# Seven block products for gate and up in three of four feed-forward blocks, with the weight sums on GpSimd

## What is computed

```python
D_FF = 2816

def swiglu(h, w1, w3, w2):
    return (jax.nn.silu(h @ w1) * (h @ w3)) @ w2

def _half_ffn(h, g, m, k, w1, w3, w2):
    y = swiglu(_modulate(h, g, m, k), w1, w3, w2)
    return h + (0.5 * m[:, :, 3 * k + 2] * y).astype(h.dtype)
```

## Time and profile before

| what | value |
|---|---|
| median of three runs | 2884.31 us |
| span of the profiled execution (its own total time is not listed) | 2881.4 us |
| granted TensorE clock, mean | 0.991 of full speed |
| TensorE busy | 2789.6 us, 97% |
| VectorE busy | 1520.7 us, 53% |
| ScalarE busy | 1126.3 us, 39% |
| GpSimd busy | 546.4 us, 19% |
| HBM read | 255.48 MB, 89 GB/s over the span |

### The profile page before, as it was taken

How to read it: one execution, slowest core, us unless ns; L and a number is a source line. 1 busy time by engine, 2 the same in 40 slices (tenths; PEclk the granted TensorE clock), 3 DMA queues, 4 the chain that set the end, 5 groups by cost and what they waited for, 6 DMA issues and landing times.

```text
span 2881.4 us, 40758 instructions
## 1 busy us (share of the span) xinstructions
PE 2789.6 (97%) x15696; PEld 2604.4 (90%) x15696; DVE 1520.7 (53%) x1919; ACT 1126.3 (39%) x1620; POOL 546.4 (19%) x264
## 2 busy tenths in 40 slices
PE   5999999999998999999999999999999999899999
PEld 5899999999986799999999999999998875788887
DVE  6974266564558668652664632222247657543332
ACT  3333134335547635331343422123324876532231
POOL 2442044210002522430442100000011520100000
PEclk8999999999999999999999999999999999999999
DMA  7443144212130014441442122212222110123232
GB/s 295 139 153 133 49 151 155 92 47 65 53 73 1 1 52 139 160 155 50 152 158 88 47 65 68 70 51 66 65 67 73 52 59 8 59 88 104 93 97 99
DMA packets 68391, 258.76 MB, mean 90 GB/s; under 512 B 7504, under 2 KB 9424, under 8 KB 67792
## 3 DMA queue, kind: packets, MB, share of 16 engines
q1 hardware_dynamic: 50736, 192.59, 20.3%
q10 hardware_dynamic: 17568, 65.02, 6.6%
HBM read 255.48 MB, written 2.10 MB: 89 GB/s over the span
## 4 chain that ended last, share of the span: by engine, by line
PE 86%; DVE 7%; issue 2%; ACT 2%; POOL 0%; DVEq 0%; POOLq 0%; ACTq 0%
PE banks L459 21%; PE banks L463 21%; PE banks L461 21%; PE banks L466 5%; PE banks L470 5%; PE banks L468 5%; DVE banks L1661 2%; PE banks L950 1%; PE banks L789 1%; DVE wl L1656 1%; PE banks L973 1%; DVE tmp L1849 1%; DVE xl L1841 1%; PE banks L873 1%; DVE nsS L2008 0%
## 5 line engine op out<-in xcount | busy, mean ns | idle before, releaser
L1079 ACT ACTIVATE wh<-raw 128x1024 fp32r<-128x1024 f32 (+1 forms) x300 | 338.8, 1129 | 1454.3 <-PE banks L463 1151.3
L459 PE MATMUL banks<-xh,wh 128*128 128x384 f32 x2608 | 671.6, 338 | 27.9 <-DVE wl L1656 15.8
L461 PE MATMUL banks<-xl,wh 128*128 128x384 f32 x2608 | 664.7, 335 | 0.0
L463 PE MATMUL banks<-xh,wl 128*128 128x384 f32 x2608 | 664.4, 335 | 0.0
L1656 DVE TENSOR_TENSOR wl<-raw,wh 128x1024 fp32r<-128x1024 f32 (+1 forms) x300 | 428.3, 1428 | 350.6 <-ACT wh L1079 349.8
L459 PEld LDWEIGHTS banks<-xh,wh 128*128 128x128 f32 x2608 | 471.7, 189 | 37.1 <-DVE wl L1656 19.0
L461 PEld LDWEIGHTS banks<-xl,wh 128*128 128x128 f32 x2608 | 473.9, 189 | 0.0
L463 PEld LDWEIGHTS banks<-xh,wl 128*128 128x128 f32 x2608 | 473.1, 189 | 0.0
L2419 POOL TENSOR_TENSOR mraw<-mraw,scb 128x1024 f32<-128x1024 f32 x120 | 316.1, 2635 | 636.2 <-DVE banks L1661 636.2
L463 PE MATMUL banks<-hh,wl 128*128 128x384 f32 x1056 | 267.9, 334 | 0.0
L461 PE MATMUL banks<-hl,wh 128*128 128x384 f32 x1056 | 267.9, 334 | 0.0
(11 more groups left out here) (368 smaller groups left out, 3240.4 us busy)
## 6 DMA issues: line engine op xcount, KB each, us to landing
raw<-in_w SPq DMA_DIRECT2D x176, 512.0 KB, 3.6
mraw<-in_wmn ACTq DMA_DIRECT2D x120, 512.0 KB, 4.4
raw<-in_w SPq DMA_DIRECT2D x64, 704.0 KB, 4.0
raw<-in_abin SPq DMA_DIRECT2D x24, 512.0 KB, 3.6
raw<-in_cdin SPq DMA_DIRECT2D x20, 512.0 KB, 3.6
mini<-in_wmn SPq DMA_DIRECT2D x9, 512.0 KB, 14.8
gmini<-in_wmn SPq DMA_DIRECT2D x2, 2048.0 KB, 21.8
raw<-in_about SPq DMA_DIRECT2D x8, 512.0 KB, 3.5
```

Of the source, the lines that this page charges most:

```text
L459: pe.matmul(bank(h), W, tokens(rh, h), start=(k == 0), stop=False)
L461: pe.matmul(bank(h), W, tokens(rl, h), start=False, stop=False)
L463: mm = pe.matmul(bank(h), L, tokens(rh, h), start=False, stop=(k == nk - 1))
L1079: act.activation(wh[slot][:, 0:nk * P], raw[slot][:, 0:nk * P], ACT.Copy).then_inc(hi_done, 1)
```

## The change

In blocks 0, 1 and 2 there are four rounds, of 4, 6, 6 and 6 chunks; in block 3 three rounds of 7, 7 and 8. The first round of each block is made as before. In the other 18 pairs of blocks 0 to 2 the two tiles of a pair are seen as a 2 x 2 matrix of blocks (gate A11 A12, up A21 A22; the second index is the half of the input features) times a 2 x 2 matrix of token blocks (even and odd blocks of 128 tokens, 384 each). The product is worked out with seven products of 4 input blocks by 384 tokens, each of 12 matmuls, in place of eight. This needs

- four sums of weight blocks, 128 x 512 each, on GpSimd (`weight_sum`: S1 = A21+A22, S2 = S1-A11, S3 = A11-A21, S4 = A12-S2), then seven weight blocks split by ScalarE and VectorE in place of two tiles;
- sums of the tokens once per block (`sums`, `sums_lo`, `first_sum_lo`), made by VectorE beside the first round;
- the results put together from the products: six additions on VectorE that read PSUM, one on GpSimd that doesn't (`first_quarter`), copies and silus by halves on ScalarE, and the hidden chunk made by halves;
- other buffers: `raw`, `wh`, `wl` shrink to 1024 columns; `raw[1]` is loaded again after the low part of S3 and `raw[0]` after the low part of A12, as those are their last readers.

The context dot products of the 120 columns go from GpSimd and ScalarE to VectorE, as a second `dot` behind the first. They are spread over blocks 0, 1 and 2: one column at each pair of a seven-product round, one at each down tile of the second and third round, two at the third and fourth pair of a block, and six beside the down tiles of the first mixer. `mraw` has two buffers. The second `gmini` load (modulation columns for the first gate) waits for the first dot products. Small semaphores are merged.

The core of the diff (TensorE, SyncE, GpSimd, ScalarE, VectorE):

```diff
-FH = FC // 2
+GROUPS = ((4, 6, 6, 6),) * 3 + ((7, 7, 8),)
+W_ORDER = ("S1", "A11", "S2", "A22", "S3", "S4", "A12")
+            def load_after_seven(t, s, src, nk):
+                slot = t % 2
+                sp.wait_ge(w_lo, w_count(s, "S3" if slot else "A12"))
+                sp.dma_start(raw[slot][:, 0:nk * P], src).then_inc(raw_landed[slot], 16)
...
+            def product(bank, name, rh, rl):
+                for k in range(4):
+                    W, L = W_HI[name][:, k * P:(k + 1) * P], W_LO[name][:, k * P:(k + 1) * P]
+                    pe.matmul(thirds(bank), W, rh(k), start=(k == 0), stop=False)
+                    pe.matmul(thirds(bank), W, rl(k), start=False, stop=False)
+                    mm = pe.matmul(thirds(bank), L, rh(k), start=False, stop=(k == 3))
+                return mm
...
+                pe.wait_ge(w_lo, w_count(s, "A11"))
+                pe.wait_ge(psum_free[1], t // 2 - 1)
+                product(P1_BANK[i % 2], "A11", *tokens(0, 0)).then_inc(p_done, 1)
+                pe.wait_ge(psum_free[0], t // 2)
+                product(P5_BANK, "S1", *tokens(0, 1)).then_inc(p_done, 1)
+                pe.wait_ge(w_lo, w_count(s, "S2"))
+                product(P6_BANK, "S2", *sums(0)).then_inc(p_done, 1)
+                if s:
+                    pe.wait_ge(comb_set, comb_count(s - 1, "C21"))
+                pe.wait_ge(w_lo, w_count(s, "S3"))
+                product(P7_BANK, "S3", *sums(1)).then_inc(p_done, 1)
+                pe.wait_ge(w_lo, w_count(s, "S4"))
+                pe.wait_ge(psum_free[1], t // 2)
+                product(P3_BANK, "S4", *tokens(4, 1)).then_inc(p_done, 1)
+                pe.wait_ge(w_lo, w_count(s, "A12"))
+                pe.wait_ge(half_set, 3 * s + 1)
+                product(P1_BANK[i % 2], "A12", *tokens(4, 0)).then_inc(mm_done, 1)
+                pe.wait_ge(comb_set, comb_count(s, "C22"))
+                product(P7_BANK, "A22", *sums(2)).then_inc(mm_done, 1)
...
+            def seven_pool(f):
+                def weight_sum(g, i, name):
+                    t, s = up_tile(f, g) + 2 * i, seven_pair(f, g, i)
+                    pool.wait_ge(raw_landed[1], 16 * (t // 2) + 16)
+                    if name != "S1":
+                        pool.wait_ge(raw_landed[0], 16 * (t // 2) + 16)
+                    if s:
+                        pool.wait_ge(w_lo, w_count(s - 1, name))
...
+                    for i in range(GROUPS[f][g]):
+                        weight_sum(g, i, "S1")
+                        weight_sum(g, i, "S2")
+                        if i:
+                            first_quarter(g, i - 1)
+                        weight_sum(g, i, "S3")
+                        weight_sum(g, i, "S4")
+                    first_quarter(g, GROUPS[f][g] - 1)
...
+            def seven_act(f, g, i):
+                weight_hi(f, g, i, "A22")
+                weight_hi(f, g, i, "S3")
+                if i:
+                    hidden_hi(f, g, i - 1, 0)
+                act.wait_ge(p_done, 5 * s + 1)
+                act.activation(p1[:], P1_BANK[i % 2], ACT.Copy).then_inc(half_set, 1)
+                weight_hi(f, g, i, "S4")
+                weight_hi(f, g, i, "A12")
+                next_mods(f, ("up", first_chunk(f, g) + i))
...
+            def last_quarter(f, g, i):
+                dve.wait_ge(mm_done, t + 2)
+                dve.tensor_tensor(half(hf[:], 0), thirds(u2), thirds(P7_BANK), ALU.add).then_inc(comb_set, 1)
+                dve.tensor_tensor(half(hf[:], 0), half(g1s[:], 0), half(hf[:], 0), ALU.mult).then_inc(hf_set, 1)
+            def seven_dve(f, g, i):
+                if i:
+                    last_quarter(f, g, i - 1)
+                weight_lo(f, g, i, "A22")
+                weight_lo(f, g, i, "S3")
+                if i:
+                    hidden_lo(f, g, i - 1, 0)
+                weight_lo(f, g, i, "S4")
+                dot_mods(f, ("up", first_chunk(f, g) + i))
+                dve.wait_ge(half_set, 3 * s + 1)
+                dve.wait_ge(p_done, 5 * s + 3)
+                dve.tensor_tensor(u2, p1[:], P6_BANK, ALU.add).then_inc(comb_set, 1)
+                dve.tensor_tensor(uv, u2, P5_BANK, ALU.add).then_inc(psum_free[0], 1)
+                weight_lo(f, g, i, "A12")
+                if not last:
+                    weight_lo(f, g, i + 1, "S1")
+                dve.wait_ge(p_done, 5 * s + 4)
+                dve.tensor_tensor(u2, u2, P7_BANK, ALU.add).then_inc(comb_set, 1)
+                dve.tensor_tensor(half(hf[:], 1), thirds(uv), thirds(P7_BANK), ALU.add).then_inc(comb_set, 1)
+                dve.wait_ge(p_done, 5 * s + 5)
+                dve.tensor_tensor(half(g1s[:], 1), thirds(uv), thirds(P3_BANK), ALU.add).then_inc(comb_set, 1)
+                if last:
+                    split_lo(t + 2, 0, n)
+                else:
+                    weight_lo(f, g, i + 1, "A11")
+                dve.tensor_tensor(half(hf[:], 1), half(g1s[:], 1), half(hf[:], 1), ALU.mult).then_inc(hf_set, 1)
+                if not last:
+                    weight_lo(f, g, i + 1, "S2")
+                hidden_lo(f, g, i, 1)
...
             add_squares(0, T)
-            prod_mods(0)
-            prod_mods(10)
+            seven_pool(0)
```

More of the change, by code:

```diff
@@ L65, with first_chunk, up_tile, down_tile @@
 N_TILES = _t
+def first_chunk(f, g):
+    return sum(GROUPS[f][:g])
+def up_tile(f, g):
+    return BASE[f"ffn{f}"] + 2 * first_chunk(f, g) + KC * g
+def down_tile(f, g):
+    return up_tile(f, g) + 2 * GROUPS[f][g]
+def seven(f, g):
+    return f < 3 and g > 0
+NSEVEN = FC - GROUPS[0][0]
+def seven_pair(f, g, i):
+    return NSEVEN * f + first_chunk(f, g) - GROUPS[f][0] + i
+_seven = [False] * N_TILES
+for _f in range(4):
+    for _g in range(len(GROUPS[_f])):
+        if seven(_f, _g):
+            for _q in range(2 * GROUPS[_f][_g]):
+                _seven[up_tile(_f, _g) + _q] = True
@@ new lines, with w_count, comb_count @@
+PLAIN = [0]
+for _v in _seven:
+    PLAIN.append(PLAIN[-1] + (not _v))
+W_ORDER = ("S1", "A11", "S2", "A22", "S3", "S4", "A12")
+def w_count(s, name):
+    return 7 * s + W_ORDER.index(name) + 1
+COMB_ORDER = ("U2", "U3", "C22", "C12", "C21")
+def comb_count(s, name):
+    return 5 * s + COMB_ORDER.index(name) + 1
+POOL_COUNT = {}
+for _f in range(3):
+    for _g in range(1, len(GROUPS[_f])):
+        for _i in range(GROUPS[_f][_g] + 1):
+            _s = seven_pair(_f, _g, _i)
+            for _key in ((_s, "S1"), (_s, "S2"), (_s - 1, "C11"), (_s, "S3"), (_s, "S4")):
+                if (_i if _key[1] == "C11" else _i < GROUPS[_f][_g]):
+                    POOL_COUNT[_key] = len(POOL_COUNT) + 1
@@ new lines, in pool_count, with mod_places @@
+def pool_count(s, name):
+    return POOL_COUNT[s, name]
+def mod_places():
+    where = []
+    for f in range(3):
+        place = {}
+        for ch in (2, 3):
+            place["up", ch] = 2
+        for ch in range(4, FC):
+            place["up", ch] = 1
+        for g in (1, 2):
+            for j in range(KC):
+                place["down", g, j] = 1
+        if f == 0:
+            place["down", 1, 2] = place["down", 2, 2] = 2
+        if f == 2:
+            place["down", 2, 2] = place["down", 2, 5] = 0
+        where.append(place)
+    m, out = 0, []
+    for f in range(3):
+        start = m
+        table = {}
+        for g, n in enumerate(GROUPS[f]):
+            for key in [("up", first_chunk(f, g) + i) for i in range(n)] + [("down", g, j) for j in range(KC)]:
+                table[key] = range(m, m + where[f].get(key, 0))
+                m += where[f].get(key, 0)
+        out.append((start, m, table))
+        if f == 0:
+            m += AB_MODS
+    assert m == 120, m
+    return out
@@ L68 @@
+W2_ROW = {}
+_rows = {}
+for _f in range(4):
+    for _g, _n in enumerate(GROUPS[_f]):
+        W2_ROW[_f, _g] = _rows.get(_n, 0)
+        _rows[_n] = W2_ROW[_f, _g] + 1
+AB_MODS = 6
+MODS = mod_places()
+AB_MOD0 = MODS[0][1]
 PCOL = {}
@@ new lines, in load_ffn @@
+            def load_ffn(f):
+                for g, n in enumerate(GROUPS[f]):
+                    t0, d = up_tile(f, g), down_tile(f, g)
+                    row = 2 * (f * FC + first_chunk(f, g))
+                    for i in range(n):
+                        src = [dr["w13"][row + 2 * i + q] for q in range(2)]
+                        if seven(f, g) and i:
+                            s = seven_pair(f, g, i)
+                            load_after_seven(t0 + 2 * i + 1, s - 1, src[1], KC)
+                            load_after_seven(t0 + 2 * i, s - 1, src[0], KC)
+                        elif f or g or i:
+                            load(t0 + 2 * i, src[0], KC)
+                            load(t0 + 2 * i + 1, src[1], KC)
+                    row2 = KC * W2_ROW[f, g]
+                    for j in range(KC):
+                        src = dr[f"w2_{n}"][row2 + j]
+                        if seven(f, g) and j < 2:
+                            load_after_seven(d + j, seven_pair(f, g, n - 1), src, n)
```

(4 more changed lines are left out.)

732 lines of the change are left out of this document (450 added, 282 removed).

## The result

The changed kernel takes **3022.61 us** (3018.68 to 3025.93) against 2884.14 for the kernel before: ratio 1.0483, 95% interval 1.0468 to 1.0498. The forecast was 2957, with a range of 2835 to 3010: the sign was right, the size was not (+138 in place of +73).

A forecast was written before the change was run, and what follows sets the result against it. TensorE bounds the kernel before; afterwards a round trip sets 18.2 us per pair, over its 14.56. Rounds +68, first down tiles +4.5, mixer +2, start -2: +72.5 on the 2881.4 span, about 2954; median 2957, range 2835 to 3010.

The forecast's parts named there:

- The exclusion: GpSimd and VectorE instructions with two SBUF inputs lock each other out; lock work is 14.4 of a pair's 14.56 us.
- the round trip: Seven-product pairs: from one A12 low part to the next, 18.2 us taken, bounds 17.0 to 19.0; TensorE waits 3.6.
- its two legs: Leg 1, A12's low part to next A11's, transfer included: 5.65 us; leg 2, A11's to A12's, with dots: 12.2 to 12.75.
- Rival 1: GpSimd's sums fall in VectorE's waits, so pairs take 14.56 us: total 2792, or 2835 half way; chance 0.24.
- Rival 3: Break-even: trip of some 16.7 us, transfers at 3.0 and S2 not holding A11: 2865 to 2895; chance 0.07.
- Rival 2: Longer trip, 19.5 us and up, from transfers at 4.4 and more and several sums keeping the lock: above 3010; chance 0.09.
- the sum over a round: Seven-product rounds of six pairs: +5.9 first, +9.2 second, +7.6 third; +22.7 us per block, +68 for three blocks.
- The four in the middle: Middle pairs of a seven-product round: each 18.2 us, the length of the trip.
- The first pair: First pair of a seven-product round: 16 us in first rounds, 19.3 behind down tiles with a column each.
- The last pair: Last pair of a round, loading nothing: 14.56 us plus 2.3 of late dots in the down tiles; none in third rounds.
- First-round down tiles: Down tiles of each block's first round: VectorE's work with token sums 27.7 of 33.3 us, unevenly, +1.5 per block.
- The start: Near the start, context products leave GpSimd and splits meet no lock: up to -4 of 15.8 us of waits, taken -2.

The follow-up runs named there:

- run 4: Changed kernel with GpSimd's four weight sums cut to 8 of 512 columns after the very first pair: 2871.4 us.
- run 5: Changed kernel with short weight sums, each followed by an idle GpSimd sum of 504 columns that nobody waits for: 2988.2 us.
- run 6: Changed kernel with the four weight sums moved from GpSimd to VectorE: 2967.3 us.
- run 7: Changed kernel with each seven-product pair's two column dots, and their load's issue on ScalarE, moved behind C12: 2956.5 us.
- run 2: Changed kernel with the two column dots of every seven-product pair reading 8 of 1024 elements: 2919.3 us.
- run 3: Changed kernel with the reload of raw[0] bringing 256 KB in place of 512 in seven-product pairs after the first of a round: 2975.6 us.
- run 8: Changed kernel with the weight sums on VectorE and the pair's column dots behind C12, both together: 2868.4 us.
- run 12: Changed kernel with the column dots of the down tiles over 8 of 1024 elements: 3001.7 us; a further kernel followed.
- run 10: Token sums moved ahead in chunks 2 and 3: changed kernel 3057.8 us; with VectorE weight sums and late dots 2904.4, or 2874.5 with the sums spread.
- last kernel of run 12: Changed kernel with weight sums and C11 on VectorE, pair dots behind C12, down tiles 6 and 7's column pairs moved to 1 and 4: 2834.5 us.
- run 9: Changed kernel with three of the four token sums of a block cut from 4.0 us to about 0.7: 3000.6 us.
- run 13: Kernel before the change, with GpSimd's context products over 8 of 1024 columns: 2876.5 us, ratio 0.9975.

## Why the prediction was right in sign and wrong in size

**Right.** The exclusion (runs 4 and 5), the round trip as what sets the pair and not VectorE's amount of work (runs 6 and 7 have more or equal work and are faster), its two legs and what stands in them (runs 2 and 3), and the two low parts named as releasers: A11's and A12's are the gaps of 1.68 and 0.97 in the steady pair. Matmuls saved, down tiles behind the rounds and the last block were costed rightly. Rivals 1 and 3 are refuted for this kernel. Rival 2 described the outcome by its total but not by its way: trips of 19.5 did not come, though its longer transfers did. A third releaser was not forecast: S3's low part, 36 us over the nine rounds.

**The failed step is the sum over a round**, +22.7 per block in the forecast, +39 measured, so +50 of the missing 65. The first pairs, the middle ones and the last ones each bring about a third of it. From first product to first product, over the nine rounds:
- The four in the middle: 18.2 forecast, 18.7 at the mean. The term that was mis-sized is the transfer of leg 1. The forecast took the 3.6 of the earlier trace rows over the 4.4 of loads that cross others, "as the transfers are of the kind of the 3.6 row". In this kernel they are not: the column load from ScalarE's queue is under way, and the reload of `raw[0]` lands after 4.2 us; in runs 7 and 8, where nothing issued by ScalarE runs beside it, after 3.6. The seven middle pairs over 19.2 us are those of the seven transfers of 5.0 to 6.4 us; why these took so long is open.
- The first pair: forecast 16 in the first rounds and 19.3 in the others; measured 17.3 and 21.5 (20.9 to 22.7). The dots of down tiles 6 and 7 were in the forecast's list, but as work that is done in order, not as what holds S1's and S2's turn (run 12: 3 us).
- The last pair: forecast "loads nothing, 14.56 plus 2.3", 16.9, and 15.3 in the third rounds by their +7.6; measured 18.8 and 17.0. It loads nothing for a next pair, but its own products still wait for the trip that began a pair earlier (about 1 us, in two of the rounds a stretch at the lower clock instead), and TensorE waits another 2.1 to 2.6 ahead of the down tiles (0.5 in the third rounds).

The estimate of 3.2 us that the forecast took from the Trainium skill ("DMA: Bandwidth & Descriptors", anatomy of one DMA) rests on a fit for transfers issued by GpSimd. SyncE issues these, and the medians measured here for its weight loads of 512 KB are 3.5 us and more.

**A term that was left out: TensorE's clock.** The forecast let the gaps cost their own length alone. The profile shows more. A gap in the changed kernel, and what follows it:

```profile
1396.71 0.41 PE L708 MATMUL banks<-th,wh 128*128 128x384 f32 x1 [2.68 <-DVE wl L2003]
1396.96 0.34 PE L709 MATMUL banks<-tl,wh 128*128 128x384 f32 x1
...
1397.76 0.52 PE L710 MATMUL banks<-th,wl 128*128 128x384 f32 x1
1398.08 0.52 PE L708 MATMUL banks<-th,wh 128*128 128x384 f32 x1
```

```profile
1394.00:1396.00 2.00, 0.03 (x1) 0.00 (x0) 0.87 (x4) 1.39 (x3) 0.00 (x0) 1.00 0.39 80
1396.00:1397.70 1.70, 0.99 (x5) 1.02 (x6) 1.58 (x3) 1.18 (x3) 0.00 (x0) 0.94 0.71 231
1397.70:1401.00 3.30, 3.30 (x12) 3.30 (x12) 3.23 (x7) 0.00 (x0) 0.54 (x1) 0.51 0.59 160
```

After an idle stretch of 2.68 us the granted clock falls to 0.51, the 1.2 GHz level, for 3.3 us, in which matmuls start every 0.32 us in place of 0.17; eleven of them lose 1.6 us. The nine rounds have 19 such stretches, in which matmuls lose 32 us. In the two rounds of the last kernel of run 12 shown above the clock is 1.00, and so it was in the three windows of the earlier trace rows.

How much of the missing 50 us is this? In the middle pairs, nothing that shows: the 7 of 36 with such a stretch take 18.4 us at the mean, the other 29 take 18.8. There the trip sets the pair, and slower products fit beside it. All nine first pairs have one, so that their share cannot be told from the trip's. In the faster kernels, where TensorE waits less, the clock does show in the time (runs 10 and 12).

**First-round down tiles: 4.5 forecast, 24 measured.** The forecast summed VectorE's work (27.7 of 33.3 us) and called the rest "uneven". What decides is order: chunk 3's sum, which the forecast had counted to the up tiles, stands ahead of the first residual update (run 9). About 10 of the 24 us are the wait ahead of the first product behind these tiles. Here I argued from amount of work, the argument that I had refused for the pairs.

**The start: -2 forecast, -13 measured**, in the other direction (run 13). A quarter of the 15.8 us of waits was taken as the most that could come back, and half of that as likely; the round's 17.4 us over its matmuls, of which these waits are only a part, was not looked at.

**The first mixer's output tiles: +2 forecast**, none seen. The mixer takes the same 454.9 us in both kernels. So the missing 65 are 50 + 20 - 11 - 2, and some 8 are spread over the kernel.

## What to carry to other kernels

GpSimd was no free engine here: an instruction of it stopped VectorE's instructions that read two operands from SBUF. Price each such instruction as a stop of the other engine, and compare with doing the work on the busy engine at its own speed. Where one engine serves a loop with a single load buffer, draw the trip from the buffer's release to its next release, ask which other loads are under way during its transfer, and put work that nobody waits for (column dots) into the transfer's shadow; 66 us came from moving two instructions and the load that feeds them, 27 from moving such dots out of the tiles ahead of a round. In a stage that is full for several tiles, ask of each tile what stands ahead of its first consumer, also for work issued a chunk earlier; the amount per stage is no answer.

## What was not expected of the hardware

- In 19 places of the nine rounds TensorE's matmuls went at half the rate for 3 to 4.5 us, in two of them for over 5, each behind a gap of 1.8 to 4.3 us (16 of these 2.5 us and more). Behind the gaps of 1.0 and 1.7 us in the steady pair the rate stayed, and so it did behind the 3.29 us at 1197.57: what decides is left open.
- The exclusion lengthens GpSimd too: its idle sum of 504 columns took 1.38 us at the mean, the changed kernel's S3 and S4 sums 1.63 and 1.74, for 1.22 alone.
- A load of 512 KB from SyncE's queue took 4.2 us with a column load from ScalarE's queue under way, 3.6 without (run 7). A transfer of half the bytes was 1.0 us shorter from issue to first reader (3.2 for 4.2) beside the same column load; the page's medians, 3.1 and 3.6, show only half of that.
